# Sums of squares of the mixed halves: four channel groups added on VectorE, two products instead of eight per tile on TensorE

## The chip, the cores and the metric

The kernel runs on one core of one Trainium2 chip. The metric is the device time of one execution in microseconds (us); the number compared is the median of several runs of the same kernel.

## What is computed

The reference is one block over 2048 tokens of 1024 channels: a mixing part (a convolution half and a state-space half, 512 channels each), then a mixture of experts. The change touches the place where the two halves are normalised, each by itself, and joined by the output projection:

```python
mixed = jnp.concatenate([rms_norm(a_out, g_out_conv[l]), rms_norm(b_out, g_out_ssm[l])], axis=-1)
o = mixed @ w_out[l]
x = x + gt_m * rms_norm(o, g_post_mix[l])
```

`rms_norm` needs, for each token and each half, the sum of the squares over 512 channels. The rest of the block follows: a second norm, the router (sigmoid scores of 64 experts, 8 chosen of 4 groups), the chosen experts and one shared expert, and the last norm.

## The kernel before

The 2048 tokens are 16 tiles (NT) of 128. Every engine runs its own written-out list of steps, and they meet at semaphores only; nothing reorders them. The stage that matters here is the loop `for i in range(NT)`, present once in each engine's program, which does the output projection of tile i while earlier tiles are routed and pass through the shared expert (tile j = i - LAG, LAG = 5).

The mixed tile lies in SBUF with the channels on the partitions, as eight groups of 128 channels by 128 tokens (the first four are one half, the last four the other). ScalarE's `square_mix(i)` (L1407) squares all 1024 elements of a partition at once into `sqb`, a single buffer. TensorE's `sums(i)` then sums over the channels: with a group of squares as the stationary operand and a column of ones as the moving one, a product leaves one number per token, and four such products are accumulated into one PSUM column for each half (L1026). VectorE's `ssn(i)` (L1820) takes the two columns, GpSimd's `rr(i)` (L2128, L2129) makes the two reciprocal roots. The projection itself (`mix_half`, L1036, 32 matmul records of 128x512 a tile) uses the unnormalised tile; the roots scale its two results, first on ScalarE (`scaled_a`, L1415), then on VectorE (`joined`, L1830).

TensorE's order in one turn i is: `mix_half(i, 0)` and `mix_half(i, 1)` (L1036), `turn_h2(i-1)` (L1048), `positions(i-2)` (L1067, L1068), `shared_gate_up(j)` (L1090), `route(i-1)` (L1058), `shared_down(j-1)` (L1090), `sums(i+1)` (L1026), `turn_h(j)` (L1112). VectorE's order is: `joined(i)` (L1830, L1824, L1834), `hidden(j)` (L1922, L1924), `shared_low(j+1)` (L1932), `ssn(i+1)` (L1820), `scaled_x1(i)` (L1842), `h_low(j)` (L1928), `dispatch(i-2)` (L1846 to L1853), `choose(i-1)` (L1793 to L1815), and in the turns 0, 1 and 2 one part of the shared expert's weights (L1971). GpSimd makes the reciprocal root of the projection's norm (L2043, L2044, awaited by L1834), adds the residual (L2140), makes the next root (awaited by L1842), the roots of `rr(i+1)`, adds a row to the normalised tile (L2148) and issues the eight indirect DMAs of `dispatch(i-2)` (L2152).

The waits that the prediction speaks of: `sums(i)` waits for the squares, for `ssn` and for the scores; `positions(i-2)` waits for the end of `choose(i-2)`; `route(i-1)` waits for `take_positions` (L1824), which stands behind L1830 on VectorE; the second half of a projection waits for `joined` of the tile before.

Of the kernel before, what the change touches and what calls it, by code (L numbers as in the profile page):

```python
# [21 lines left out]
ALU = mybir.AluOpType  # L22
# [14 lines left out]
NT = T // P  # L37
CC = 512
CT = CC // P
# [29 lines left out]
class Chain:  # L69
# [13 lines left out]
    def do(self, *instructions):  # L83
        for ins in instructions:
            self.add(ins)
        self.sync()
# [6 lines left out]
def build(nc, A, out):  # L93
    ctx = ExitStack()
    with ctx:
        def sb(name, shape, dt=F32):
            return ctx.enter_context(nc.sbuf_tensor(name, shape, dt))

        def sem(name):
            return ctx.enter_context(nc.semaphore(name))  # L100
# [80 lines left out]
        one = sb("one", [P, 1])  # L181
# [16 lines left out]
        psm = ctx.enter_context(nc.psum_tensor("psm", [P, 8, 512], F32))  # L198
# [52 lines left out]
        s_wdown_in = sem("wdown_in")  # L251
        s_ob_full = sem("ob_full")
        s_sqm_ready = sem("sqm_ready")
        s_x1_out0 = sem("x1_out0")
        s_x1_out1 = sem("x1_out1")
        s_s1_ready = sem("s1_ready")
# [193 lines left out]
        V, SC, TE, PO, SY = nc.vector, nc.scalar, nc.tensor, nc.gpsimd, nc.sync  # L450
# [4 lines left out]
        sqb = us[:, 2048:3072].rearrange("p (k t) -> p k t", k=KD)  # L455
# [87 lines left out]
        def _(sp):  # L543
# [66 lines left out]
            def store_bo(key):  # L610
                n = BON[key]
                sp.wait_ge(s_bo_full, n + 1)
                o = [s_bo_out0, s_bo_out1][n % 2]
                src = bo[:, n % 2, :].rearrange("p (a t) -> p a t", a=4)
                if key[0] == "ln":
                    SY.dma_start(mix_d[key[1] * TPH + key[2], :, 0:CT, :], src).then_inc(o, 16)
                else:
                    _, h, b, q = key
                    i0 = h * TPH + 4 * b
                    SY.dma_start(mix_d[i0:i0 + 4, :, CT + q, :].rearrange("i p t -> p i t"), src).then_inc(o, 16)  # L620
# [197 lines left out]
        def _(pe):  # L818
# [37 lines left out]
            for q in range(CT):  # L856
                m = TE.transpose(b[:, 8 * G + q * TAPS:8 * G + (q + 1) * TAPS], cwn[:, q * P:(q + 1) * P], ident[0:TAPS, 0:TAPS])
# [5 lines left out]
            for n in range(NADA):  # L863
                for c in range(4):
                    m = TE.transpose(b[:, 4 * n + c:4 * n + c + 1], segs[n][:, c * P:(c + 1) * P], ident[0:1, 0:1])
# [150 lines left out]
                ada(n)  # L1016

            def sums(i):
                pe.wait_ge(s_sqm_ready, i + 1)
                if i:  # L1020
                    pe.wait_ge(s_ssn_ready, i)
                if i >= 2:
                    pe.wait_ge(s_sc_ready, i - 1)
                for f in range(2):
                    for q in range(CT):
                        m = TE.matmul(psm[:, 5, f:f + 1], sqb[:, f * CT + q, :], one[:, :], start=(q == 0), stop=(q == CT - 1))  # L1026
                m.then_inc(s_ss_full, 1)

            def mix_half(i, f, parts=range(2)):
# [105 lines left out]
            for i in range(TPH + 2):  # L1135
# [7 lines left out]
                if i == 6:  # L1143
                    mix_half(0, 0, [1])
            sums(0)
            pe.wait_ge(s_tp_free, len(tpk))
            pe.wait_ge(s_wr_in, 32)
            for i in range(NT):
                j = i - LAG
                if i:  # L1150
                    mix_half(i, 0)
                mix_half(i, 1)
                if i >= 1:
                    turn_h2(i - 1, max(j - 1, 0))
                if i >= 2:
                    positions(i - 2)
                if j >= 0:
                    shared_gate_up(j)
                if i >= 1:
                    route(i - 1)  # L1160
                if j >= 1:
                    shared_down(j - 1, i)
                if i + 1 < NT:
                    sums(i + 1)
                if j >= 0:
                    turn_h(j, 4)
# [51 lines left out]
            q = pe.value_load(ordi[0:1, bass.ds(nb - 1, 1)], min_val=1, max_val=E)  # L1218
# [355 lines left out]
        def _(dve):  # L1574
            ch = Chain(dve, s_dve_step)
            tt, ts, stt = V.tensor_tensor, V.tensor_scalar, V.scalar_tensor_tensor
            do, add, sync = ch.do, ch.add, ch.sync
# [108 lines left out]
            for n in range(8):  # L1686
                lr, li = (L[:, w, n + 1].unsqueeze(2).to_broadcast([P, G, HG]) for w in range(2))
                t = [PT[2 + n % 2][:, j * 512:(j + 1) * 512].rearrange("p (g h) -> p g h", g=G) for j in range(2)]
# [128 lines left out]
            def ssn(i):  # L1817
                c0 = 16 * (i % 2)
                dve.wait_ge(s_ss_full, i + 1)
                ts(st[:, c0:c0 + 2], psm[:, 5, 0:2], 1.0 / CC, EPS, ALU.mult, ALU.add).then_inc(s_ssn_ready, 1)  # L1820

            def take_positions(i):
                dve.wait_ge(s_pos_full, i + 1)
                tt(dm, psm[:, 5, 320:320 + E], ebase, ALU.add).then_inc(s_dm_ready, 1)  # L1824

            def joined(i):
                c0 = 16 * (i % 2)
                dve.wait_ge(s_ob_full, i + 1)
                dve.wait_ge(s_oa_ready, i + 1)
                stt(ob, psm[:, 2:4, :].rearrange("p a n -> p (a n)"), st[:, c0 + 3:c0 + 4], ob, ALU.mult, ALU.add).then_inc(s_o_ready, 1)  # L1830
                if i >= 2:
                    take_positions(i - 2)
                dve.wait_ge(s_ro_ready, i + 1)
                stt(ob, ob, st[:, c0 + 6:c0 + 7], row[0], ALU.mult, ALU.mult).then_inc(s_t_ready, 1)  # L1834

            def scaled_x1(i):
                c0 = 16 * (i % 2)
                dve.wait_ge(s_r1_ready, i + 1)
                if i >= 2:
                    dve.wait_ge(s_h2t_full, i - 1)  # L1840
                    dve.wait_ge([s_h2_out0, s_h2_out1][i % 2], 16 * (i // 2))
                stt(h2b[:, i % 2, :], xb[:, i % 2, :], st[:, c0 + 9:c0 + 10], row[1], ALU.mult, ALU.mult).then_inc(s_ha_ready, 1)  # L1842

            def dispatch(i):
                dve.wait_ge(s_dm_ready, i + 1)
                do(tt(dm, dm, sel, ALU.mult))  # L1846
                do(V.max(d8, dm))
                do(tt(eqb, dm.unsqueeze(1).to_broadcast([P, TOPK, E]), d8.unsqueeze(2).to_broadcast([P, TOPK, E]), ALU.is_equal),
                   ts(qi, d8, -1.0, None, ALU.add))
                do(tt(eqb, eqb, gw.unsqueeze(1).to_broadcast([P, TOPK, E]), ALU.mult),  # L1850
                   ts(bi, qi, 7, None, ALU.arith_shift_right), ts(qi, qi, BLK - 1, None, ALU.bitwise_and))
                do(V.tensor_reduce(pay[:, i * TOPK:(i + 1) * TOPK, 1], eqb, AX.X, ALU.add), V.tensor_copy(bf_, bi), V.tensor_copy(qf, qi))
                stt(di[:, i * TOPK:(i + 1) * TOPK], qf, float(NCOL), bf_, ALU.mult, ALU.add).then_inc(s_pay_ready, 1)  # L1853
                dve.wait_ge(s_pay_ready, i + 1)
# [65 lines left out]
            def hidden(b, w=1.0, bank=0):  # L1920
                dve.wait_ge(s_sig_ready, b + 1)
                tt(htmp, psm[:, bank, 0:DE], sigb, ALU.mult).then_inc(s_hm_ready, 1)  # L1922
                dve.wait_ge(s_hm_ready, b + 1)
                stt(hs, htmp, w, psm[:, bank, DE:2 * DE], ALU.mult, ALU.mult).then_inc(s_h_full, 1)  # L1924

            def h_low(b, bank=1):
                dve.wait_ge(s_ht_high, b + 1)
                tt(hlo[:, :], psm[:, bank, 0:DE], hhi[:, :], ALU.subtract).then_inc(s_ht_ready, 1)  # L1928

            def shared_low(j):  # L1930
                dve.wait_ge(s_xt_high, j + 1)
                tt(xlo[:, :], h2r[j % 4], xhi[:, :], ALU.subtract).then_inc(s_xt_ready, 1)  # L1932
# [9 lines left out]
            def routed_step(b):  # L1942
# [6 lines left out]
                    split_low((on & 1) * WSLOT, on * NGC)  # L1949
                h_low(b)  # L1950

            ssn(0)
            for i in range(NT):
                j = i - LAG
                joined(i)
                if j >= 0:
                    hidden(j, bank=4)
                if j + 1 >= 0:
                    shared_low(j + 1)
                if i + 1 < NT:  # L1960
                    ssn(i + 1)
                scaled_x1(i)
                if j >= 0:
                    h_low(j, 4)
                if i >= 2:
                    dispatch(i - 2)
                if i >= 1:
                    choose(i - 1)
                if i < 3:
                    dve.wait_ge(s_ws_hi, i + 1)  # L1970
                    tt(wlo[:, WSLOT + i * WC:WSLOT + (i + 1) * WC], wsr, whi[:, WSLOT + i * WC:WSLOT + (i + 1) * WC], ALU.subtract).then_inc(s_ws_lo, 1)  # L1971
            j = NT - LAG
            hidden(j)
            shared_low(j + 1)
            take_positions(NT - 2)
            dispatch(NT - 2)
            h_low(j)
            choose(NT - 1)
            hidden(j + 1)
            shared_low(j + 2)  # L1980
            take_positions(NT - 1)
            count_blocks()
            h_low(j + 1)
# [273 lines left out]
```

## Time and profile before

| | |
|---|---|
| Median of 3 runs | 2850.31 us (2847.86 to 2851.01) |
| The profiled execution, its own time | 2835.12 us |
| Its span, first to last instruction | 2833.4 us |
| TensorE busy (matmul) | 2616.1 us, 92% of the span |
| TensorE weight loads | 1884.1 us, 66% |
| VectorE busy | 1568.9 us, 55% |
| GpSimd busy | 1467.4 us, 52% |
| ScalarE busy | 1146.0 us, 40% |
| Mean granted TensorE clock | 0.963 of full speed |

The busy shares are averages over the whole program; the stage with the 16 tiles lies between 700 us and about 1100 us of the span, and the loop over the experts' blocks fills most of what follows. The profiled execution is 15.2 us shorter than the median of the timed runs. In a profile, one product of two float32 operands shows as two weight loads (LDWEIGHTS) and two MATMUL records, so the eight products of `sums` are 16 of each.

### The profile page before, as it was taken

What the parts mean: (1) busy time and instruction counts of PE and PEld (TensorE: products, weight loads), DVE (VectorE), ACT (ScalarE), POOL (GpSimd) and SP (SyncE); (2) the same over time, 40 slices, a digit from 0 to 9 for tenths busy, and PEclk for the clock granted to TensorE, in tenths of its full rate; (3) what the DMA queues carried; (4) which work ended last, traced back from release to release, by engine and by line L of the source; (5) the groups of instructions that cost most, each with busy time, mean ns of one, the idle gap of its engine ahead of it and who ended that gap; (6) DMA issues with size and microseconds to landing.
All of it is one profiled execution on the core that took longest, in us unless ns stands there. A gap on an engine that the chain in (4) does not pass through costs nothing.

```text
span 2833.4 us, 49475 instructions
## 1 busy us (share of the span) xinstructions
PE 2616.1 (92%) x11400; PEld 1884.1 (66%) x11401; DVE 1568.9 (55%) x2559; ACT 1146.0 (40%) x1534; POOL 1467.4 (52%) x1756
## 2 busy tenths in 40 slices
PE   6999997996999999799999999999999999999980
PEld 1754663522556666687878788878778777787760
DVE  6379987993566667433433333444445544454425
ACT  4132312323323322344444444455555555555532
POOL 2012206125465665444555555556776777766756
PEclk8999999997999999899999999999999999999995
DMA  8152604463323221757777778788889988899877
GB/s 272 63 98 89 215 0 64 157 226 130 127 89 105 90 97 61 275 133 198 197 197 200 215 192 241 203 223 259 259 262 272 283 263 261 258 266 265 255 214 273
DMA packets 304952, 534.61 MB, mean 189 GB/s; under 512 B 38597, under 2 KB 204485, under 8 KB 304120
## 3 DMA queue, kind: packets, MB, share of 16 engines
q1 hardware_dynamic: 250248, 352.77, 37.7%
q0 software_dynamic: 51472, 173.70, 25.6%
q10 hardware_dynamic: 3168, 7.34, 0.7%
q8 instruction: 33, 0.54, 0.1%
q14 instruction: 31, 0.25, 0.0%
HBM read 395.75 MB, written 138.00 MB: 188 GB/s over the span
## 4 chain that ended last, share of the span: by engine, by line
PE 38%; issue 16%; POOL 10%; POOLq 6%; DVE 2%; DMA 1%; ACT 0%; SPq 0%; ACTq 0%
PE psm L1090 27%; PE psm L1036 6%; PE psm L1083 2%; POOL arena L2170 2%; POOL arena L2167 2%; POOL st L2160 2%; POOLq L2166 2%; POOLq L2188 1%; POOLq L2187 1%; POOLq L2179 1%; PE psm L1058 1%; PE psm L1026 1%; POOL st L2044 1%; POOL arena L2180 1%; PE psm L1112 1%
## 5 line engine op out<-in xcount | busy, mean ns | idle before, releaser
L1090 PE MATMUL psm<-whi,xhi 128*128 (+1 forms) x1424 | 575.7, 404 | 28.5 <-issue 15.3
L1090 PE MATMUL psm<-whi,xlo 128*128 (+1 forms) x1424 | 558.5, 392 | 0.0
L1090 PE MATMUL psm<-wlo,xhi 128*128 (+1 forms) x1424 | 556.9, 391 | 0.0
L1922 DVE TENSOR_TENSOR arena<-psm,arena 128x256 f32<-128x256 f32 x178 | 75.4, 424 | 597.6 <-ACT arena L1457 597.6
L1764 DVE SCALAR_TENSOR_TENSOR arena<-arena,cw 128x1024 f32<-128x1024 f32 x240 | 335.6, 1398 | 8.6
L2175 POOL TENSOR_TENSOR wlo<-raw,whi (+1 forms) x64 | 330.6, 5166 | 18.5 <-ACT whi L1489 18.5
L1090 PEld LDWEIGHTS psm<-whi,xhi 128*128 128x128 f32 x1424 | 268.5, 189 | 99.8 <-issue 48.7
L1090 PE MATMUL psm<-whi,hhi 128*128 (+1 forms) x712 | 294.6, 414 | 19.7 <-POOL wlo L2175 13.5
L2184 POOL DMA_INDIRECT acc_d<-arena x162 | 278.0, 1716 | 58.7 <-issue 54.5
L1090 PEld LDWEIGHTS psm<-whi,xlo 128*128 128x128 f32 x1424 | 268.4, 188 | 59.0
L1090 PEld LDWEIGHTS psm<-wlo,xhi 128*128 128x128 f32 x1424 | 269.3, 189 | 51.3
L1457 ACT ACTIVATE arena<-psm 128x256 f32<-128x256 f32 x178 | 68.2, 383 | 572.5 <-PE psm L1090 571.9
L1938 DVE TENSOR_TENSOR wlo<-raw,whi (+1 forms) x256 | 296.4, 1219 | 1.7 <-ACT whi L1485 1.7
L1090 PE MATMUL psm<-whi,hlo 128*128 (+1 forms) x712 | 280.8, 394 | 0.0
L1090 PE MATMUL psm<-wlo,hhi 128*128 (+1 forms) x712 | 279.8, 393 | 0.0
L1463 ACT COPY arena<-psm 128x1024 f32<-128x1024 f32 x162 | 164.1, 1013 | 217.4 <-PE psm L1090 167.9
L1485 ACT CAST whi<-raw (+1 forms) x256 | 249.4, 1051 | 2.2 <-DMA raw<-in_we_up_dram 2.2
L1036 PE MATMUL psm<-arena 128*128 128x512 f32 x512 | 236.6, 622 | 4.9 <-DMA arena<-mix_d 2.5
L1918 DVE TENSOR_TENSOR xlo<-psm,xhi 128x1024 fp32r<-128x1024 f32 x163 | 199.5, 1224 | 66.6 <-ACT xhi L1453 65.6
L946 PE MATMUL psm<-arena 128*128 128x512 f32 x512 | 225.8, 598 | 9.2 <-DMA arena<-in_w_in_dram 9.2
L2170 POOL DMA_INDIRECT arena<-h_d,arena x165 | 188.0, 1140 | 35.4 <-issue 20.8
L1453 ACT CAST xhi<-psm 128x1024 fp32r<-128x1024 f32 x163 | 165.5, 1015 | 82.6 <-PE psm L1083 82.6
(357 smaller groups left out, 3885.9 us busy)
## 6 DMA issues: line engine op xcount, KB each, us to landing
raw<-in_we_gate_dram SPq DMA_DIRECT2D x64, 1024.0 KB
raw<-in_we_up_dram SPq DMA_DIRECT2D x64, 1024.0 KB
raw<-in_we_down_dram SPq DMA_DIRECT2D x64, 1024.0 KB, 5.1
arena<-in_w_ada_dram SPq DMA_DIRECT2D x12, 2048.0 KB
arena<-in_x_dram SPq DMA_DIRECT2D x32, 512.0 KB, 5.4
h_d<-arena SPq DMA_DIRECT2D x17, 512.0 KB, 2.6
arena<-in_w_in_dram SPq DMA_DIRECT2D x16, 512.0 KB, 6.2
mix_d<-bo SPq DMA_DIRECT2D x32, 256.0 KB, 2.3
```

The costliest lines, as they stand in the source:

```text
L946: m = TE.matmul(b[:, :], wz_conv(q)[:, w, k, :], hT[:, k, b2 * 512:(b2 + 1) * 512], start=(k == 0), stop=(k == KD - 1))
L1036: m = TE.matmul(psm[:, 2 * f + c, :], mixb[:, i % 2, f * CT + q, :], wout[:, f * CT + q, c * 512:(c + 1) * 512], start=(q == 0), stop=(q = ...
L1090: m = TE.matmul(o, a, w, start=(n == 0), stop=(n == len(todo) - 1))
L1453: SC.copy(xhi[:, :], psm[:, 2:4, :].rearrange("p a n -> p (a n)")).then_inc(s_xt_high, 1)
L1463: SC.copy(yb[w], psm[:, 4:6, :].rearrange("p a n -> p (a n)")).then_inc(s_y_act, 1)
L1485: SC.copy(whi[:, bass.ds(slot + c * GC, GC)], raw[:, bass.ds(slot + c * GC, GC)]).then_inc(s_whi_ready, 1)
L1764: m = stt(o, v[:, q, k:k + HT], cw[:, q, k:k + 1], o, ALU.mult, ALU.add)
L1918: tt(xlo[:, :], psm[:, 2:4, :].rearrange("p a n -> p (a n)"), xhi[:, :], ALU.subtract).then_inc(s_xt_ready, 1)
L1938: m = tt(wlo[:, bass.ds(slot + c * GC, GC)], raw[:, bass.ds(slot + c * GC, GC)], whi[:, bass.ds(slot + c * GC, GC)], ALU.subtract)
L2170: PO.indirect_dma_start(xg[w], None, h2_d, bass.IndirectOffsetOnAxis(idxg[w], 0)).then_inc([s_xr_in0, s_xr_in1][w], 16)
L2175: PO.tensor_tensor(wlo[:, bass.ds(slot + WG, FE * D)], raw[:, bass.ds(slot + WG, FE * D)], whi[:, bass.ds(slot + WG, FE * D)], ALU.subtrac ...
L2184: PO.indirect_dma_start(acc_d, bass.IndirectOffsetOnAxis(idxs, 0), yb[w], None, compute_op=ALU.add).then_inc(s_ya_out, 16)
```

## The change

`sums(i)` makes one product for each half instead of four. What it multiplies is the first group of each half, in which VectorE has added the four groups beforehand: the new `squares_joined(i)` adds groups 2 and 3 to groups 0 and 1 in both halves at once (128 partitions x 512 elements), then group 1 to group 0 (128 x 256), in place. TensorE waits for the second addition (`s_sqq_ready`) where it waited for the squares.

```diff
             def sums(i):
-                pe.wait_ge(s_sqm_ready, i + 1)
+                pe.wait_ge(s_sqq_ready, i + 1)
                 if i:
                     pe.wait_ge(s_ssn_ready, i)
                 if i >= 2:
                     pe.wait_ge(s_sc_ready, i - 1)
                 for f in range(2):
-                    for q in range(CT):
-                        m = TE.matmul(psm[:, 5, f:f + 1], sqb[:, f * CT + q, :], one[:, :], start=(q == 0), stop=(q == CT - 1))
+                    m = TE.matmul(psm[:, 5, f:f + 1], sqb[:, f * CT, :], one[:, :], start=True, stop=True)
                 m.then_inc(s_ss_full, 1)
...
+            def squares_joined(i):
+
+                dve.wait_ge(s_sqm_ready, i + 1)
+                sq = sqb.rearrange("p (f q) t -> p f q t", f=2)
+                do(tt(sq[:, :, 0:2], sq[:, :, 0:2], sq[:, :, 2:4], ALU.add))
+                tt(sq[:, :, 0], sq[:, :, 0], sq[:, :, 1], ALU.add).then_inc(s_sqq_ready, 1)
...
+            squares_joined(0)
             ssn(0)
             for i in range(NT):
                 j = i - LAG
+                if i + 1 < NT:
+                    squares_joined(i + 1)
                 joined(i)
```

On VectorE, between `choose` of one turn and `joined` of the next, in the middle of the loop, the rows before are these (`arena` is the region in which nearly all buffers lie; `ob_full` and `oa_ready` are the two halves of the projection):

```order
L1814 RECIPROCAL arena<-arena 128x1 [waits dve_step]
L1815 TENSOR_SCALAR arena<-arena 128x64 [waits dve_step]
L1830 SCALAR_TENSOR_TENSOR arena<-psm,st,arena 128x1024 [waits oa_ready,ob_full]
L1824 TENSOR_TENSOR arena<-psm,arena 128x64 [waits pos_full]
L1834 SCALAR_TENSOR_TENSOR arena<-arena,st 128x1024 [waits ro_ready]
```

and of the change, where `joined` begins at L1837:

```order
L1814 RECIPROCAL arena<-arena 128x1 [waits dve_step]
L1815 TENSOR_SCALAR arena<-arena 128x64 [waits dve_step]
L1826 TENSOR_TENSOR arena<-arena 128x2x256 [waits sqm_ready]
L1827 TENSOR_TENSOR arena<-arena 128x2x128 [waits dve_step]
L1837 SCALAR_TENSOR_TENSOR arena<-psm,st,arena 128x1024 [waits oa_ready,ob_full]
L1831 TENSOR_TENSOR arena<-psm,arena 128x64 [waits pos_full]
L1841 SCALAR_TENSOR_TENSOR arena<-arena,st 128x1024 [waits ro_ready]
```

The two additions stand ahead of the first instruction of `joined`, 16 times in all; what stood behind it keeps its order, its line numbers 7 higher.

On TensorE, at the end of a turn, the rows before are:

```order
L1090 MATMUL psm<-whi,hlo 128x512
L1026 MATMUL psm<-one,arena 128x1 [waits sc_ready,ssn_ready,sqm_ready]
L1026 MATMUL psm<-one,arena 128x1 x7
L1112 MATMUL psm<-ident,arena 128x128 [waits h_full]
L1112 MATMUL psm<-ident,arena 128x128
L1036 MATMUL psm<-arena 128x512 [waits oa_ready,mix_in1]
```

and of the change:

```order
L1090 MATMUL psm<-whi,hlo 128x512
L1026 MATMUL psm<-one,arena 128x1 [waits sc_ready,ssn_ready,sqq_ready]
L1026 MATMUL psm<-one,arena 128x1
L1112 MATMUL psm<-ident,arena 128x128 [waits h_full]
L1112 MATMUL psm<-ident,arena 128x128
L1036 MATMUL psm<-arena 128x512 [waits oa_ready,mix_in1]
```

Two products stand where eight stood, and the semaphore of VectorE's second addition where that of ScalarE's squares was. Nothing else of TensorE's list moves.

## Rows read from the trace of the kernel before

**Rows 1.** Windows: busy us and records of each engine, granted clock, DMA share, GB/s.

```profile
700.00:1075.00 375.00, 366.10 (x1443) 231.86 (x1444) 223.57 (x639) 114.02 (x167) 221.02 (x231) 0.95 0.29 99
...
1250.00:2700.00 1450.00, 1417.92 (x6863) 1159.16 (x6862) 655.56 (x842) 736.74 (x903) 921.94 (x1100) 1.00 0.83 238
```

**Rows 2.** Chain that ended last, 640 to 1300 us: start, us, what.

```profile
885.01 1.68 PE psm L1026 x16
886.96 13.73 PE psm L1036 x32
...
911.75 1.68 PE psm L1026 x16
```

**Rows 3.** Timeline, weight loads, 880 to 935 us: start, us, engine, line, what, count.

```profile
884.62 1.98 PEld L1026 LDWEIGHTS psm<-one,arena 128*128 128x128 f32 x16
...
886.44 0.28 PEld L1112 LDWEIGHTS psm<-ident,arena 128*128 128x128 f32 x2
```

**Rows 4.** Timeline, 899 to 904.5 us, VectorE and GpSimd: in brackets idle before, releaser.

```profile
899.08 0.25 DVE L1815 TENSOR_SCALAR arena<-arena 128x64 f32<-128x64 f32 x1
...
900.74 1.28 DVE L1830 SCALAR_TENSOR_TENSOR arena<-psm,st,arena 128x1024 f32<-128x1024 f32 x1 [1.40 <-PE psm L1036]
...
904.03 0.19 POOL L2043 TENSOR_SCALAR st<-st 128x1 f32<-128x1 f32 x1
```

**Rows 5.** Timeline and window of an early tile's sums.

```profile
733.15 3.49 PEld L1026 LDWEIGHTS psm<-one,arena 128*128 128x128 f32 x16 [0.51 <-issue]
736.59 15.45 PE L1036 MATMUL psm<-arena 128*128 128x512 f32 x32
...
730.00:737.00 7.00, 5.81 (x33) 5.71 (x34) 1.57 (x3) 2.54 (x5) 3.09 (x3) 0.70 0.67 224
```

**Rows 6.** Groups of VectorE by form, 700 to 1100 us: busy us, mean ns.

```profile
L1850 DVE TENSOR_TENSOR arena<-arena 128x512 f32<-128x512 f32 x13 | 9.0, 692 | 0.4
...
L1922 DVE TENSOR_TENSOR arena<-psm,arena 128x256 f32<-128x256 f32 x11 | 4.7, 423 | 13.7 <-ACT arena L1457 13.7
```

**Rows 7.** Timeline of the first tiles, 703 to 824 us.

```profile
703.53 1.22 PE L1036 MATMUL psm<-arena 128*128 128x512 f32 x1 [2.37 <-ACT ly L1382]
...
724.39 4.33 DVE L1971 TENSOR_TENSOR wlo<-ws_raw,whi 128x2048 fp32r<-128x2048 f32 x1 [0.54 <-ACT whi L1535]
...
728.85 1.28 DVE L1830 SCALAR_TENSOR_TENSOR arena<-psm,st,arena 128x1024 f32<-128x1024 f32 x1
...
746.83 2.28 DVE L1971 TENSOR_TENSOR wlo<-ws_raw,whi 128x2048 fp32r<-128x2048 f32 x1
...
752.08 1.28 DVE L1830 SCALAR_TENSOR_TENSOR arena<-psm,st,arena 128x1024 f32<-128x1024 f32 x1 [2.96 <-PE psm L1036]
...
773.99 2.29 DVE L1971 TENSOR_TENSOR wlo<-ws_raw,whi 128x2048 fp32r<-128x2048 f32 x1
...
776.19 1.28 DVE L1830 SCALAR_TENSOR_TENSOR arena<-psm,st,arena 128x1024 f32<-128x1024 f32 x1
...
777.75 1.97 PE L1058 MATMUL psm<-arena 128*128 128x64 f32 x16 [1.32 <-DVE arena L1824]
...
822.84 0.26 DVE L1815 TENSOR_SCALAR arena<-arena 128x64 f32<-128x64 f32 x1
...
823.42 0.19 PE L1067 MATMUL psm<-arena,tri 128*128 128x64 bf16 x1
```

**Rows 8.** Timeline, VectorE's L1842 of the last two tiles.

```profile
1074.02 1.28 DVE L1842 SCALAR_TENSOR_TENSOR arena<-arena,st 128x1024 f32<-128x1024 f32 x1
...
1098.36 1.28 DVE L1842 SCALAR_TENSOR_TENSOR arena<-arena,st 128x1024 f32<-128x1024 f32 x1 [1.36 <-POOL st L2044]
```

**Rows 9.** Timeline, 775 to 791 us: VectorE and GpSimd side by side.

```profile
775.21 1.89 POOL L2152 DMA_INDIRECT rows_d<-arena  x1 [0.30 <-issue]
...
788.08 2.34 POOL L2148 TENSOR_TENSOR arena<-arena 128x1024 f32<-128x1024 f32 x1
788.13 2.83 DVE L1848 TENSOR_TENSOR arena<-arena 128x512 f32<-128x512 f32 x1
```

More of the change, by code:

```diff
@@ L253, in build @@
         s_sqm_ready = sem("sqm_ready")
+        s_sqq_ready = sem("sqq_ready")
         s_x1_out0 = sem("x1_out0")
```

## The prediction

> **What bounds the kernel now.** I began with the windows, since a busy share over the whole program says nothing of one stage. In the stretch of the 16 tiles TensorE is busy 366.1 of 375 us, VectorE 223.6 and GpSimd 221.0 [rows 1]. The loop over the experts' blocks, 1250 to 2700 us, is TensorE's too (1417.9 of 1450). The change doesn't touch it, and it starts when the tiles are done: what the tiles gain should reach the end whole.
>
> Next the chain that ended last, because "busy" may hide a wait. From turn 7 on it is TensorE alone, turn after turn: the sums, the projection, and back to the sums, 911.75 - 885.01 = 26.74 us later [rows 2]. The 16 records of the sums are a link of it. So in a steady turn each microsecond taken from them should be a microsecond of the kernel, as long as no other loop is as long as TensorE's.
>
> **What is removed.** In a steady turn the first weight load of the sums starts at 884.62 and the next line's at 886.44 [rows 3]. That is 1.82 us for 16 records, 0.114 us each, though each streams a single column: the weight load sets the pace. Two products are four records, 12 fewer: 12 x 0.114 = 1.37 us less in a turn at full clock. In the early tiles the granted clock falls, to 0.70 on average in 730 to 737 us, which is part 2.4, part 1.2 GHz; there the sums run from 733.15 to the projection at 736.59, 3.44 us, of which 12/16 are 2.6 us [rows 5]. The Trainium skill (TensorE: Matmul & The Clock Gate, "Back-to-back issue gap") gives about 60 cycles, 25 ns, for a matmul of up to 64 columns; by an estimate from that page 12 of those would save only 0.3 us a turn, 3 us in ten turns. The trace speaks against pricing these products so; it agrees with the Trainium skill's section on LDWEIGHTS (same page), which counts the 128 columns of the stationary operand, an estimate of 107 ns.
>
> **What is added.** Two additions on VectorE in each turn: 128x512 like L1850, 0.69 us, and 128x256 like L1922, 0.42 us [rows 6]. With some 0.05 us between them, my guess for a pair that waits on each other, that is 1.16 us. Below, they can't cost less than nothing where VectorE is idle. Above, each could be held by a GpSimd operation, as L1848 was: 2.83 us instead of 0.69, side by side with L2148 [rows 9], so 2.1 us more.
>
> *A steady turn.* The additions wait for squares that ScalarE made a turn earlier, and TensorE needs them only at the end of the turn; neither wait should be seen. What stands behind them on VectorE is `joined`. L1815 ends at 899.33 and L1830 starts at 900.74 after 1.40 us of idling for TensorE [rows 4]. 1.16 us fit into 1.40, since both neighbours move with TensorE: L1815 hangs on the end of the sums, and from there to the end of the projection nothing is shortened. The cover is thin. If it goes, `joined` is a few tenths late, and its readers next: the root on GpSimd, which starts at 904.03 only because the eight DMAs have just ended [rows 4]. So that is hidden too.
>
> *The other loop.* VectorE and GpSimd form a loop by way of L1842, dispatch, the DMAs, the two roots and back. On the last tile no sums hold L1842 back, and it starts 1098.36 - 1074.02 = 24.34 us after the one before [rows 8]. That is what this loop needs when left alone. The additions aren't in it: they come after the step that releases the DMAs. TensorE's new turn, 26.74 - 1.37 = 25.37 us, still is 1.0 us longer. So steady turns gain 1.37 us each.
>
> *The early tiles.* Here it is otherwise. The sums of tile 0 end long before 703.53, when the projection starts after waiting for ScalarE [rows 7]: no gain. In turns 0 to 2 VectorE also splits a part of the shared weights (L1971), and in two of them `joined` follows back to back: 728.72 to 728.85, and 776.28 less the overlap to 776.19 [rows 7]. There every 1.16 us is on VectorE's path. Walking through: L1830 of tile 1 goes from 728.85 to 730.0. That of tile 2 had waited 2.96 us for TensorE; VectorE is now free at 749.11 + 1.16 + 1.16 = 751.4 at the latest, TensorE earlier, so it goes from 752.08 to 751.4, and to 751.0 where the delay of tile 1 is partly swallowed by a step that had slack. I take 1.0 us earlier. That of tile 3 comes again right behind L1971, so 1.16 later against that: 776.19 becomes about 776.3. `route` at 777.75, whose wait ended with VectorE's L1824 [rows 7], stays where it is. The savings of the sums of tiles 1, 2 and 3 on TensorE (1.4 + 2.6 + 2.6 us) are thus turned into waiting. The sums of tiles 4 and 5 save some 2.3 us each, and TensorE then waits again: L1067 at 823.42 comes right behind the end of `choose` (822.84 + 0.26) [rows 7]. That end hangs on the second loop, not on the additions, and moves with tile 2's `joined`, plus a little from the sums: 1.2 us earlier. That is all that is left of five turns at this point. The bounds are 0 (the additions meet a GpSimd operation once) and 1.4 + 4 x 2.6 = 11.8 us (TensorE keeps all of it).
>
> *The sum.* From there on ten sums, of tiles 6 to 15, at full clock: 10 x 1.37 = 13.7 us. With the 1.2 us: **14.9 us**. The profiled execution, 2835.1 us with a span of 2833.4, would become 2820.2. It lies 15.2 us under the median of the runs; the gain taken from the median gives 2850.3 - 14.9 = **2835.4 us**. Behind the last tile everything hangs on L1842 of tile 15, which moves with the rest.
>
> **Rivals.**
>
> *TensorE keeps the early gain.* If the clock does not fall where the stretch of short records gets shorter, or the VectorE chain has slack that I don't see, up to 11.8 instead of 1.2 us: gain 25.5, 2825 us. Half of it is more plausible: 2830. Against it: L1830 back to back behind L1971, twice [rows 7].
>
> *The second loop becomes the bound.* It needs 24.34 us alone and has 1.0 us of room. During the DMAs a GpSimd issue took 1.89 instead of 0.96 us while VectorE ran a long two-input operation [rows 9]. If the additions hold one issue for as long as they last, the loop is 24.34 + 1.11 = 25.45 and nearly nothing is lost. If each costs what L1848 lost, 2.1 us, but one only, it is 26.5, and a turn gains 0.2 instead of 1.37: gain 3, 2847 us, no change that can be told.
>
> *Slower: both additions meet GpSimd, in the loop.* Two stalls of 2.1 us that also hold the DMAs make 24.34 + 4.2 = 28.6 us; above 26.74, so from 2.4 us of stall on, the turn is longer than before, and ten turns cost 10 x 1.8 = 18 us: 2868 us. For it: both of them read two SBUF operands, as L1848 does. Against it: they run while GpSimd only issues DMAs, and L1850, of the same shape, mostly runs in 0.69. The Trainium skill (SBUF — State Buffer, "two separate sides") says that a VectorE operation with two SBUF inputs and a GpSimd operation exclude one another for a whole instruction, whichever starts first. By that rule, rows 9 are this lock, and it speaks against putting more such additions on VectorE; the time it would give is that of this rival and the one above.
>
> *The change doesn't do what it says.* The instruction lists show two products for eight and one more wait. Only if TensorE waited for the additions would the gain be undone, and they end some 10 us before the sums begin. I give that no chance of its own.
>
> **Chances.** Forecast (gain 9 to 19 us) 0.72; early gain kept at least in part (above 19) 0.10; gain between 6 and 9 for a thinner cover 0.07; second loop as the bound, no change, 0.07; slower 0.04. What a measurement of this kernel can tell is about 0.2%, 5.7 us. So faster 0.89, the same 0.07, slower 0.04. The range of 2827 to 2844 us leaves out the strongest form of the first rival and the last two.
>
> **What would show it.** In the profile after: the sums with 4 weight loads and about 0.46 us in a steady turn; the turn from sums to sums at 25.4 us; L1830, now L1837, with next to no idling ahead of it; the two additions at 0.69 and 0.42 us; L1842, now L1849, still held by the sums and not by GpSimd. In the first tiles: the same L1058 near 777.7 us with a longer wait for VectorE, L1067 near 822 us. I am wrong if the steady turn is longer than 25.6 us, if TensorE waits in steady turns, or if an addition takes over 1 us there. A gain under 9 us with a steady turn of 25.4 would say that the early tiles lost more than they had.

## The result and the profile after

| | before | change |
|---|---|---|
| Median of 22 runs each | 2848.61 us | 2828.32 us |
| The profiled execution, its own time | 2835.12 us | 2823.84 us |
| Its span | 2833.4 us | 2822.1 us |
| Mean granted TensorE clock | 0.963 | 0.963 |

The ratio of the times is 0.9945, 95% interval 0.9931 to 0.9959: 15.7 us less, between 12 and 20 us, taken from 2849 us. That is an effect of about half a percent, clear of the noise. The two medians lie 20.3 us apart. The forecast was 14.9 us less, 2835.4 us in a range of 2827 to 2844; the measured median of 2828.3 is inside, near the low end.

A time of the whole program is a blunt tool here: single runs of the change lie between 2816.7 and 2856.1 us. So the main measure of what follows is a length inside the profile, called **the stage**: from the start of the first instruction of `joined` on tile 0 (L1830 before, L1837 after) to the start of the last L1842 (L1849 after), on tile 15. It holds every turn that the change touches except the sums of tile 0. It is 1098.36 - 713.33 = 385.03 us before and 1081.37 - 711.40 = 369.97 us with the change: 15.06 us less. The change profiled once more gave 370.03 us.

The chain that ended last, with the change, at the place of [rows 2] (start, us, what):

```profile
879.36 13.73 PE psm L1036 x32
893.09 0.87 PE psm L1048 x8
...
894.02 5.57 PE psm L1090 x24
899.59 1.73 PE psm L1058 x16
901.33 2.82 PE psm L1090 x12
904.15 0.34 PE psm L1026 x4
904.49 0.28 PE psm L1112 x2
904.76 13.73 PE psm L1036 x32
```

The chain is still TensorE's, without a wait of another engine in it, and a turn is 904.76 - 879.36 = 25.40 us; it was 26.74. The sums are a link of 0.34 us, where they were one of 1.68 [rows 2]. The timeline shows them too, and what VectorE does (rows picked from the timelines of the engines; start, us, engine, line, what; in brackets the idle time before and its releaser):

```profile
891.49 0.25 DVE L1815 TENSOR_SCALAR arena<-arena 128x64 f32<-128x64 f32 x1
891.62 0.96 POOL L2162 DMA_INDIRECT rows_d<-arena  x1 [0.30 <-issue]
891.66 0.68 DVE L1826 TENSOR_TENSOR arena<-arena 128x512 f32<-128x512 f32 x1
892.38 0.42 DVE L1827 TENSOR_TENSOR arena<-arena 128x256 f32<-128x256 f32 x1
...
893.13 1.28 DVE L1837 SCALAR_TENSOR_TENSOR arena<-psm,st,arena 128x1024 f32<-128x1024 f32 x1 [0.33 <-issue]
...
897.31 1.29 DVE L1841 SCALAR_TENSOR_TENSOR arena<-arena,st 128x1024 f32<-128x1024 f32 x1 [2.77 <-POOL st L2054]
...
903.76 0.64 PEld L1026 LDWEIGHTS psm<-one,arena 128*128 128x128 f32 x4
...
904.24 0.28 PEld L1112 LDWEIGHTS psm<-ident,arena 128*128 128x128 f32 x2
...
904.52 0.16 DVE L1820 TENSOR_SCALAR st<-psm 128x2 f32<-128x2 f32 x1 [2.32 <-PE psm L1026]
...
904.63 1.28 DVE L1849 SCALAR_TENSOR_TENSOR arena<-arena,st 128x1024 f32<-128x1024 f32 x1
```

Three things are to be seen. The sums take 904.24 - 903.76 = 0.48 us from their first weight load to the next line's, where they took 1.82 [rows 3]. The additions take 0.68 and 0.42 us and fit where VectorE had idled 1.40 us [rows 4]; 0.33 us of it are left. And L1849 follows `ssn` at once: it is held by the sums, not by GpSimd's root.

The first tiles (same columns) answer to [rows 7]. What was L1971 is L1981 here: inside VectorE's loop over the tiles, and in all that stands behind it, line numbers are 10 higher than before, not 7.

```profile
745.30 2.29 DVE L1981 TENSOR_TENSOR wlo<-ws_raw,whi 128x2048 fp32r<-128x2048 f32 x1
747.50 0.69 DVE L1826 TENSOR_TENSOR arena<-arena 128x512 f32<-128x512 f32 x1
...
748.22 0.42 DVE L1827 TENSOR_TENSOR arena<-arena 128x256 f32<-128x256 f32 x1
748.56 1.28 DVE L1837 SCALAR_TENSOR_TENSOR arena<-psm,st,arena 128x1024 f32<-128x1024 f32 x1
```

```profile
766.83 1.04 PE L1048 MATMUL psm<-ident,arena 128*128 128x128 f32 x8
...
770.30 0.20 PE L1067 MATMUL psm<-arena,tri 128*128 128x64 bf16 x1 [2.44 <-issue]
...
773.42 1.28 DVE L1837 SCALAR_TENSOR_TENSOR arena<-psm,st,arena 128x1024 f32<-128x1024 f32 x1
...
774.98 3.64 PE L1058 MATMUL psm<-arena 128*128 128x64 f32 x16 [4.44 <-DVE arena L1831]
...
819.09 0.25 DVE L1815 TENSOR_SCALAR arena<-arena 128x64 f32<-128x64 f32 x1
...
819.40 0.20 PE L1067 MATMUL psm<-arena,tri 128*128 128x64 bf16 x1 [1.04 <-issue]
```

On tile 2 the chain L1981, additions, `joined` has no gap any more. In the turn of tile 3 TensorE waits twice, 2.44 us for the end of `choose` and 4.44 us for L1831, where it waited 1.32 us in that turn before [rows 7]: what it saved in the sums it now spends, nearly all of it, waiting for VectorE. The clock falls in the second wait, and the 16 records of L1058 take 3.64 instead of 1.97 us. The windows (busy us and records of PE, PEld, DVE, ACT, POOL, then granted clock, DMA share, GB/s) show full speed until 771, and 0.53 from 771 to 775 us, after TensorE had been busy 0.23 us of the three before. Over the whole place it is 0.62 on average, mostly the lower level of 1.2 GHz:

```profile
768.00:771.00 3.00, 0.23 (x2) 0.11 (x2) 2.76 (x12) 0.92 (x1) 2.39 (x3) 1.00 0.55 176
771.00:775.00 4.00, 0.02 (x1) 0.05 (x1) 3.79 (x5) 0.27 (x1) 3.08 (x4) 0.53 0.01 1
...
768.00:786.00 18.00, 10.85 (x31) 7.12 (x32) 11.25 (x22) 4.38 (x7) 13.39 (x14) 0.62 0.23 73
```

The rest of the program is where single runs differ. From the last L1842 or L1849 to the end of the span it is 1735.0 us before, 1740.7 us with the change and 1747.6 us in its second profile, with the same instructions. That swing of 12.6 us is nearly as large as the effect. The start swings too: the stage begins between 707.3 and 713.3 us in the nine profiles of this document, and the three kernels with eight products (710.1, 713.1 and 713.3) don't stand apart from the others. So the two profiled executions are only 11.3 us apart: the stage gave 15.06, an earlier start 1.93, and the rest took 5.7 back.

### The profile page after: what moved, and what is told of

Its sections match the earlier page's. It is cut to its first block, busy times and chain, and to the rows that moved or that the text cites. A ratio compares the mean times of both kernels' runs of the same rounds, so it can differ in the third digit from the quotient of the medians.

```text
span 2822.1 us, 49123 instructions
## 1 busy us (share of the span) xinstructions
PE 2591.8 (92%) x11208; PEld 1859.5 (66%) x11209; DVE 1587.0 (56%) x2591; ACT 1145.8 (41%) x1534; POOL 1471.3 (52%) x1756
## 4 chain that ended last, share of the span: by engine, by line
PE 26%; issue 20%; POOL 12%; POOLq 9%; DVE 2%; DMA 1%; ACT 0%; SPq 0%; ACTq 0%; DVEq 0%
PE psm L1090 19%; PE psm L1036 4%; POOL arena L2180 3%; POOL arena L2177 3%; POOL st L2170 2%; POOLq L2176 2%; POOLq L2198 2%; PE psm L1083 2%; POOLq L2197 1%; POOLq L2189 1%; POOL arena L2190 1%; POOL st L2054 1%; POOL acc_d L2194 1%; POOL st L2202 1%; POOL st L2053 1%
## 5 line engine op out<-in xcount | busy, mean ns | idle before, releaser
L1935 DVE TENSOR_TENSOR hlo<-psm,hhi 128x256 fp32r<-128x256 f32 x178 | 75.0, 421 | 221.8 <-ACT hhi L1478 216.2
```

## The experiments

All of them change the kernel with the change unless said otherwise. The stage and the steady turn are read from one profile each, the same way.

| kernel | additions | products a turn | stage, us | steady turn, us |
|---|---|---|---|---|
| before | none | 8 | 385.03 | 26.74 |
| the change | ahead of `joined` | 2 | 369.97 | 25.40 |
| the change again | ahead of `joined` | 2 | 370.03 | 25.40 |
| `e1_adds_only` | ahead of `joined` | 8 | 391.18 | 26.74 |
| `e2_no_adds` | none | 2 | 367.74 | 25.40 |
| `e3_moved` | inside `joined` | 2 | 367.77 | 25.40 |
| `e4_three_pairs` | ahead of `joined`, three pairs | 2 | 379.35 | 25.40 |
| `e5_half` | one, inside `joined` | 4 | 374.41 | 25.85 |
| `e6_moved_adds_only` | inside `joined` | 8 | 385.12 | 26.74 |

**The change again**, on the chip of the next three runs.

> The change as it is, on the chip of the other runs of this call, to compare them with. Stage 370 us, steady turn 25.4 us, ratio to before 0.993 to 0.996.

Stage 370.03 us; ratio to before 0.9932 (0.9907 to 0.9957). The stage repeats to 0.1 us, the whole time does not: its seven runs lie between 2818.0 and 2831.4 us.

**The additions alone.** TensorE makes each product four times.

```diff
                 for f in range(2):
-                    m = TE.matmul(psm[:, 5, f:f + 1], sqb[:, f * CT, :], one[:, :], start=True, stop=True)
+                    for q in range(CT):
+                        m = TE.matmul(psm[:, 5, f:f + 1], sqb[:, f * CT, :], one[:, :], start=True, stop=True)
```

> The two additions as in the change, but TensorE makes each of the two products four times over, so eight again (same result, 16 weight-load records a turn). The stage is read in the profile from the first L1830/L1837 to the last L1842/L1849: 385.0 us before, 370.0 with the change. My theory: the additions alone cost nothing in a steady turn (26.74 us as before) and only lengthen VectorE's path in the first tiles: stage 385 to 389 us, time equal to before within 0.2%. Rival, the additions disturb GpSimd or the projection's readers in every turn: steady turn over 27.2 us, stage over 392 us. Rival, the gain of the change does not come from the records taken from TensorE: then this kernel is as fast as the change.

Steady turn 26.74 us, as before to the last digit: the additions cost nothing there. Ratio to before 1.0009 (0.9987 to 1.0030). But the stage is 391.18 us, 6.1 us more than before and 2.2 more than the upper end of what I expected. Measured from the first `joined`, that of tile 1 comes 0.9 us later than before, that of tile 2 1.7, that of tile 3 2.7: three delays by the additions of about 0.9 us each. The next turn, from tile 3 to tile 4, takes 25.97 instead of 23.06 us, 2.9 us more by itself, and all turns after it add 0.5. In the profile of this kernel (L1059, L1027 and L1832 are what L1058, L1026 and L1831 are in the change):

```profile
780.23 3.65 PE L1059 MATMUL psm<-arena 128*128 128x64 f32 x16 [4.01 <-DVE arena L1832]
...
784.25 3.49 PEld L1027 LDWEIGHTS psm<-one,arena 128*128 128x128 f32 x16 [0.56 <-issue]
```

and its window from just before that L1059 on, then that of the kernel before from just before its L1058 on:

```profile
780.00:794.00 14.00, 13.37 (x40) 9.62 (x41) 7.37 (x12) 3.57 (x6) 10.02 (x9) 0.51 0.21 75
```

```profile
777.50:791.50 14.00, 13.35 (x47) 8.65 (x48) 6.53 (x9) 3.47 (x6) 9.63 (x10) 0.76 0.27 99
```

VectorE is late, TensorE waits 4.01 us for it, the granted clock goes to 0.51 for 14 us where it was 0.76, and the sixteen-record groups, of `route` and of the sums, take 3.5 us and more each. From the start of `route` to the start of the projection it is 7.46 us (780.23 to 787.69) instead of 5.42 (777.75 to 783.17), 2.0 of the 2.9 us; the rest falls in the projection, which also runs longer at the lower clock (0.50 in 788 to 792 us, where before has 0.83 in 786 to 790). I had counted the delay and not what the clock makes of it.

**No additions.**

```diff
             def sums(i):
-                pe.wait_ge(s_sqq_ready, i + 1)
+                pe.wait_ge(s_sqm_ready, i + 1)
...
-                ts(st[:, c0:c0 + 2], psm[:, 5, 0:2], 1.0 / CC, EPS, ALU.mult, ALU.add).then_inc(s_ssn_ready, 1)
+                ts(st[:, c0:c0 + 2], psm[:, 5, 0:2], 1.0 / P, EPS, ALU.mult, ALU.add).then_inc(s_ssn_ready, 1)
...
-            squares_joined(0)
...
-                if i + 1 < NT:
-                    squares_joined(i + 1)
                 joined(i)
```

> Two products a turn and no additions: the sums take only the first 128 of each half's 512 channels and divide by 128 instead of 512, so three quarters of the squares are left out. My theory: steady turn 25.4 us as with the change, and in the first tiles VectorE's path is shorter by one pair of additions (1.1 us) in each of tiles 1 to 3, so the stage is 2 to 4 us shorter than with the change, 366 to 368 us. Rival, the additions are hidden everywhere: 370.0 us. Rival, the early tiles lose their gain to the clock and not to VectorE: 370 us too, with joined of tile 3 coming no earlier.

Stage 367.74 us, 2.2 us under the change; steady turn the same 25.40. So the additions still cost 2.2 us in the change, all of it in the first turns. `joined` of tiles 1, 2 and 3 comes 1.0, 2.1 and 3.2 us earlier than in the change, each measured from the first; a microsecond of that is lost again by tile 7. This speaks against both rivals. Since the kernel leaves out most of the squares its results differ, and with them what the experts get: TensorE has 11392 matmul records in it instead of 11208. Its whole time, 2872.0 us in a single run, is not comparable; its stage is.

**The additions moved** behind L1837 and L1831, where VectorE waits for GpSimd's root.

```diff
-                if i + 1 < NT:
-                    squares_joined(i + 1)
+                if i == 0:
+                    squares_joined(1)
                 joined(i)
...
                 if i >= 2:
                     take_positions(i - 2)
+                if 1 <= i < NT - 1:
+                    squares_joined(i + 1)
                 dve.wait_ge(s_ro_ready, i + 1)
```

> The change with the additions at another place on VectorE: behind the first instruction of joined and the positions, ahead of the wait for GpSimd's root, where VectorE waited 2.1 to 3.2 us in every turn (for tile 1 they stay where they are). My theory: they are then hidden in the early tiles too: joined of tiles 1, 2 and 3 comes 1.1, 2 and 3 us earlier against the tile before it, steady turn 25.4 us, stage 366 to 368 us, time 2 to 4 us under the change's. Rival, they hold GpSimd's root or TensorE's sums there: stage 370 us or more.

Stage 367.77 us: what was reached without any addition, to 0.03 us. The gain is in the first turns, where `joined` of tiles 1, 2 and 3 now starts right behind L1983, the part of the shared weights (L1981 of the change):

```profile
722.58 1.27 DVE L1837 SCALAR_TENSOR_TENSOR arena<-psm,st,arena 128x1024 f32<-128x1024 f32 x1
...
742.29 1.28 DVE L1837 SCALAR_TENSOR_TENSOR arena<-psm,st,arena 128x1024 f32<-128x1024 f32 x1
...
766.04 1.28 DVE L1837 SCALAR_TENSOR_TENSOR arena<-psm,st,arena 128x1024 f32<-128x1024 f32 x1
```

The first `joined` starts at 707.26, so they come 15.32, 35.03 and 58.78 us after it, where the change has 16.38, 37.16 and 62.02: 1.06, 2.13 and 3.24 us earlier, as expected. A steady turn shows where the additions now lie (L1843 is L1841 of the change):

```profile
886.79 1.28 DVE L1837 SCALAR_TENSOR_TENSOR arena<-psm,st,arena 128x1024 f32<-128x1024 f32 x1 [1.38 <-PE psm L1036]
887.99 0.21 DVE L1831 TENSOR_TENSOR arena<-psm,arena 128x64 f32<-128x64 f32 x1
888.12 0.68 DVE L1826 TENSOR_TENSOR arena<-arena 128x512 f32<-128x512 f32 x1
888.83 0.43 DVE L1827 TENSOR_TENSOR arena<-arena 128x256 f32<-128x256 f32 x1
891.04 1.28 DVE L1843 SCALAR_TENSOR_TENSOR arena<-arena,st 128x1024 f32<-128x1024 f32 x1 [1.78 <-issue]
```

The 1.38 us of idling ahead of `joined` are back, and 1.78 us are left ahead of L1843. The ratio to before is 0.9936 (0.9915 to 0.9958), median 2827.4 us beside 2827.0 us for the change on the same chip. A difference of 2.2 us is 0.08% and can't be told in the whole time; the profile tells it.

**Three pairs of additions.**

```diff
                 do(tt(sq[:, :, 0:2], sq[:, :, 0:2], sq[:, :, 2:4], ALU.add))
+                for _ in range(2):
+                    do(tt(sq[:, :, 2:4], sq[:, :, 2:4], sq[:, :, 2:4], ALU.max))
+                    do(tt(sq[:, :, 2], sq[:, :, 2], sq[:, :, 3], ALU.max))
                 tt(sq[:, :, 0], sq[:, :, 0], sq[:, :, 1], ALU.add).then_inc(s_sqq_ready, 1)
```

> The change with three pairs of additions in the same place, two of them on channel groups whose sums are not needed (same result), so 2.2 to 2.3 us more on VectorE in each turn. It tests how thick the cover of a steady turn is. My theory: joined comes about 2 us late, but what follows waits 2.8 us for GpSimd's root anyway and the second loop has 1 us of room, so the steady turn grows by at most 0.5 us (25.4 to 25.9 us) while the first six turns lose 5 to 9 us: stage 375 to 384 us. Rival, the cover was only the 0.2 us of idle time ahead of joined: steady turn 27.4 to 27.7 us, stage over 390 us.

In the last steady turns 25.40 us, not a tenth more, and the stage 379.35 us, as expected. The cover is thicker than the gap ahead of `joined` suggests. The timeline of this kernel, first in the turns after the early ones, then in a steady turn (L1840 is `joined`, L1844 is L1841 of the change, L1852 is L1849):

```profile
912.58 1.28 DVE L1852 SCALAR_TENSOR_TENSOR arena<-arena,st 128x1024 f32<-128x1024 f32 x1 [0.55 <-POOL st L2057]
...
1001.88 1.04 PE L1048 MATMUL psm<-ident,arena 128*128 128x128 f32 x8
...
1003.69 0.43 DVE L1830 TENSOR_TENSOR arena<-arena 128x256 f32<-128x256 f32 x1
1004.04 1.28 DVE L1840 SCALAR_TENSOR_TENSOR arena<-psm,st,arena 128x1024 f32<-128x1024 f32 x1
...
1007.46 1.28 DVE L1844 SCALAR_TENSOR_TENSOR arena<-arena,st 128x1024 f32<-128x1024 f32 x1 [2.02 <-POOL st L2057]
...
1013.47 0.16 DVE L1820 TENSOR_SCALAR st<-psm 128x2 f32<-128x2 f32 x1 [1.19 <-PE psm L1026]
1013.58 1.28 DVE L1852 SCALAR_TENSOR_TENSOR arena<-arena,st 128x1024 f32<-128x1024 f32 x1
```

In the steady turn `joined` starts 2.16 us after L1048, where it started 0.20 us after it in the change: about 2.0 us late. L1844 is then only 1.2 us late, because 0.8 went into the wait for GpSimd's root (2.02 us are left of 2.77), and what is left of the delay goes into VectorE's wait for the sums ahead of L1820 (1.19 us are left of 2.32). TensorE waits for nothing, and L1852 is still held by the sums. It is otherwise in the turns before: from tile 4 to tile 9 L1852 comes every 24.8 us and the row at 912.58 waits for GpSimd's root. There VectorE is late from the first turns and catches up with TensorE at the pace of the second loop. With three pairs that loop needs 24.84 us, 0.5 more than the 24.34 of [rows 8], and 0.56 less than TensorE's 25.40. The prediction's sentence that the additions aren't in this loop does not hold for three pairs. This kernel's whole time was 2852.3 us in a single run, beside 2839.3 us for before.

**One addition, four products**, at the hidden place.

```diff
-                do(tt(sq[:, :, 0:2], sq[:, :, 0:2], sq[:, :, 2:4], ALU.add))
-                tt(sq[:, :, 0], sq[:, :, 0], sq[:, :, 1], ALU.add).then_inc(s_sqq_ready, 1)
+                tt(sq[:, :, 0:2], sq[:, :, 0:2], sq[:, :, 2:4], ALU.add).then_inc(s_sqq_ready, 1)
...
-                    m = TE.matmul(psm[:, 5, f:f + 1], sqb[:, f * CT, :], one[:, :], start=True, stop=True)
+                    for q in range(2):
+                        m = TE.matmul(psm[:, 5, f:f + 1], sqb[:, f * CT + q, :], one[:, :], start=(q == 0), stop=(q == 1))
```

> One addition (128x512) and four products a turn (8 weight-load records instead of 4), with the addition at the hidden place of the moved version (367.8 us of stage, 25.4 us steady turn). My theory, each record costs 0.114 us whatever it streams and the additions are hidden there: steady turn 25.4 + 4 x 0.114 = 25.85 us, stage 367.8 + 9 x 0.45 + up to 2 for the early turns = 371.8 to 374 us. Rival, the first product of the sums carries most of the cost (a fixed cost of the group, not of the record): steady turn under 25.6 us.

The chain of this kernel (L1027 are the sums, L1037 the projection):

```profile
880.46 0.79 PE psm L1027 x8
881.24 0.28 PE psm L1113 x2
...
906.31 0.79 PE psm L1027 x8
```

906.31 - 880.46 = 25.85 us. With 4, 8 and 16 records the steady turn is 25.40, 25.85 and 26.74 us: 0.113 us for a record over the first step, 0.111 over the second. The cost goes with the records. A fixed part of the group, which these differences alone can't show, is small: with four records the sums take 0.48 us to the next line's weight load, 0.12 each. The stage, 374.41 us, is 0.4 us above what I had named. The single timed run took 2834.8 us, beside 2839.3 us for before.

**The moved additions with eight products.** The edit is that of the additions alone, made to the moved version.

> The moved additions with eight products again (each of the two made four times): the counterpart of the run that had the additions ahead of joined, 391.2 us of stage against 385.0 before. My theory: those 6.1 us came from VectorE's path in the first turns and from TensorE's clock, which falls while TensorE waits for it; at the hidden place both go, so the stage is 385.0 to 386 us and the steady turn 26.74 us. Rival, an addition costs something wherever it stands (the waits of its own, GpSimd held): stage 388 us or more.

Stage 385.12 us, 0.1 us above before, steady turn 26.74. The 6.1 us of the first such kernel belonged to the place, not to the work. The single timed run took 2835.9 us, beside 2849.3 us for before, which says more about the scatter of the rest of the program than about the stage.

## Why the prediction was right

**What bounds the kernel.** Right. TensorE's list sets the turn before and after, and what the stage gained, 15.06 us, agrees with the 15.7 us (12 to 20) of the whole time.

**The price of a record, 0.114 us, and 1.37 us a turn.** Measured 1.34 us (26.74 - 25.40), and 0.111 to 0.113 us a record by the three counts of products. The nine turns from tile 6 to tile 15 gave 9 x 1.34 = 12.1 us.

**The additions, 0.69 + 0.42 us and 0.05 between them.** Measured 0.68 and 0.42; from the start of the first to the start of `joined` 1.06 us where `joined` follows at once (747.50 to 748.56). The estimate of 1.16 was a little high.

**Hidden in a steady turn.** Shown, by the additions alone (26.74 us unchanged) and by two kernels with and without additions (25.40 us both). I called the cover thin. That was too cautious: behind the 1.40 us ahead of `joined` stand two more waits of VectorE, for GpSimd's root and for the sums. With three pairs, 2.4 us more from the first to the last addition, the idle time ahead of `joined` took 0.4 us of it, the first of these waits 0.8 and the second 1.1.

**Nearly nothing gained in the early tiles.** The mechanism is right: TensorE's savings became waiting for VectorE. The size was a little off. Measured from the first `joined`, L1067 in the turn of tile 5 comes 110.1 us after it before and 108.0 us with the change, 2.1 us earlier; I had said 1.2. L1058 behind the wait for L1831 comes 0.8 us earlier (64.4 to 63.6 us); I had said it would stay. The step that was mis-sized is `joined` of tile 2, from which I took the end of `choose` in the turn of tile 5: it comes 1.6 us earlier (38.75 to 37.16 after the first) and not 1.0. Of the delay of tile 1, 0.9 us, only 0.4 was left where L1981 of the next turn starts, and the pair takes 1.06 instead of 1.16 us. That makes 0.6 of the 0.9 us. The other 0.3 is a misreading of [rows 7]: before, L1067 at 823.42 was not held by `choose`. It starts 0.88 us after L1048 (822.54), as in a steady turn, and its row has no wait; `choose` had ended 0.3 us earlier. Only with the change does TensorE wait for `choose` there (1.04 us), with L1067 0.06 us behind its end. In the turn of tile 6 L1067 comes 3.0 us earlier (134.6 to 131.6), where my sum had 2.6, because that turn gained 1.0 us instead of 1.37: TensorE waited there once more for the end of `choose` (L1067 starts 1.20 us after L1048, in a steady turn 0.87). Not foreseen is that TensorE's longer wait costs clock as well (3.64 instead of 1.97 us for one group), in that turn.

**The sum.** 14.9 us forecast; 15.06 us in the stage, 15.7 us (12 to 20) in the ratio of the times. That the stage fits to 0.2 us is in part luck: 0.9 us more than forecast by the turn of tile 5, 0.4 less in the next turn and 0.3 less in the nine steady ones (12.1 instead of 12.3 us) nearly cancel. The absolute forecast, 2835.4 us, was 7.1 us too high: 1.7 because the median of before came down from 2850.3 to 2848.6 us with more runs, and 5.4 because the medians of 22 runs differ by 20.3 us, more than the ratio of the same runs says. Single runs of the change scatter over some 40 us. Read by the medians alone the gain would have passed for that of the first rival (above 19 us); it is the stage that decides.

**The rivals.** TensorE kept 2.1 us of up to 11.8 by the turn of tile 5, so the first rival did not come. The second loop was not the bound, though with three pairs of additions it was within 0.6 us of being it. The slower case did not come: beside GpSimd's DMA issues an addition took 0.68 us. The lock that it rests on did show, twice, ahead of the stage and at harmless places. In the profile of the change, the first addition for tile 0 takes 1.38 us and that for tile 1 0.92 us, where each meets a GpSimd operation that began before it:

```profile
690.41 1.27 POOL L2104 TENSOR_TENSOR bo<-ly,arena 128x512 f32<-128x512 f32 x1
...
690.84 1.38 DVE L1826 TENSOR_TENSOR arena<-arena 128x512 f32<-128x512 f32 x1
...
702.79 1.27 POOL L2104 TENSOR_TENSOR bo<-ly,arena 128x512 f32<-128x512 f32 x1 [2.31 <-ACT arena L1386]
...
703.69 0.92 DVE L1826 TENSOR_TENSOR arena<-arena 128x512 f32<-128x512 f32 x1 [6.31 <-ACT arena L1407]
```

They end at 692.22 and 704.61, each 0.54 to 0.55 us after GpSimd's operation (691.68 and 704.06), and so did L1848 in [rows 9] (790.96 after 790.42). All seven profiles with additions show both. The Trainium skill (SBUF — State Buffer, "two separate sides") says that of a VectorE operation with two SBUF inputs and a GpSimd operation that reads SBUF the one that starts later is blocked until the other has ended. The trace agrees with it in these three places. In the turns with dispatch the additions lie beside DMA issues only, and the issue at 891.62 took 0.96 us like its neighbours.

## What to carry to other kernels

In this kernel a product that streams one column cost its weight load: what counted was the number of records, 0.11 us each, and not the columns streamed. Trading TensorE's records for work of another engine pays while that engine is idle at the place where the new work stands; which place it is must be read for the first turns apart from the steady ones. If an engine waits for a third one in the middle of its step, put the new work just ahead of that wait: here that made the additions free to 0.1 us over the whole stage, where at the head of the step they cost 2.2 us with two products and 6.1 us with eight.

## What was not expected

- A late VectorE costs TensorE more than the delay. With the additions ahead of `joined` and eight products three delays of about 0.9 us each were followed by one turn that lost 2.9 us, with the granted clock at 0.51 over 14 us; with 0.5 more behind it that makes 6.1 us. With the additions moved the loss was 0.1 us.
- The stage repeats to 0.1 us between two profiles of the same kernel, while the rest of the program, with the same instructions, took 1735.0 to 1761.9 us in the eight profiles of kernels that compute the same. Which part of it swings was not looked into and stays open. An effect of a few microseconds in a program like this is to be read inside the profile.
